# A decoder trunk with a top-2-of-8 expert layer: first-sweep row capacity of an expert 96 instead of 128

## What is computed

```python
def moe_swiglu(h, w_router, w_gate, w_up, w_down):
    logits = (x @ w_router)                       # x: 256 tokens x 1024
    top_logit, top_idx = lax.top_k(logits, 2)     # each token goes to 2 of 8 experts
    gates = softmax(top_logit)
    ...
    # expert e: ( silu(x_e @ w_gate[e]) * (x_e @ w_up[e]) ) @ w_down[e], 1024 -> 3584 -> 1024
    # out[token] += gate * y
```

## Time and profile before

| | us |
|---|---|
| median of 3 runs | 1450.31 (1448.35 to 1453.87) |
| the profiled execution, its own time | 1451.46 |
| its span, first to last instruction | 1449.7 |
| TensorE busy | 1418.1 (98%) |
| weight loads of TensorE | 1202.5 (83%) |
| VectorE busy | 1116.5 (77%) |
| ScalarE busy | 944.7 (65%) |
| mean granted TensorE clock | 0.993 of full |

### The profile page before, as it was taken

The page is one execution under the profiler, slowest core; times in us unless marked ns, Lnnn a source line. Parts: engine busy times, 40 slices in busy tenths (PEclk is TensorE's granted clock), DMA queues, the critical chain, the costliest instruction groups (busy, mean ns, idle before and its releaser), DMA issues.

```text
span 1449.7 us, 19532 instructions
## 1 busy us (share of the span) xinstructions
PE 1418.1 (98%) x7348; PEld 1202.5 (83%) x7348; DVE 1116.5 (77%) x865; ACT 944.7 (65%) x866; POOL 52.8 (4%) x78
## 2 busy tenths in 40 slices
PE   8999999999999999999999999999999999999997
PEld 8887899998887888888888888888888888888885
DVE  5565545456775898798888889879888888987987
ACT  5654444434664877687677777767768768677773
POOL 1000100000000500000000000000000000000002
PEclk9999999999999999999999999999999999999999
DMA  9734675555531599999999999999999999999993
GB/s 287 260 125 130 225 262 175 183 196 189 189 117 59 191 398 395 395 396 395 393 359 395 397 349 392 398 350 389 395 393 348 396 393 348 393 398 364 389 396 127
DMA packets 205253, 446.72 MB, mean 308 GB/s; under 512 B 8448, under 2 KB 42400, under 8 KB 205200
## 3 DMA queue, kind: packets, MB, share of 16 engines
q1 hardware_dynamic: 200144, 428.34, 80.3%
q0 software_dynamic: 5056, 17.66, 3.5%
HBM read 432.86 MB, written 13.11 MB: 308 GB/s over the span
## 4 chain that ended last, share of the span: by engine, by line
PE 91%; DVE 4%; ACT 3%; DMA 1%; issue 1%; SPq 1%; DVEq 0%; ACTq 0%
PE ps L1686 28%; PE ps L1688 28%; PE ps L1687 28%; PE ps L2300 2%; DMA raw<-in_w_mem_kv_dram 1%; ACT w_hi L593 1%; DVE w_lo L1058 1%; ACT sc L637 0%; PE ps L2294 0%; PE ps L1835 0%; DVE small L1105 0%; PE ps L1712 0%; DVE act_lo L1071 0%; PE ps L1804 0%; PE ps L2243 0%
## 5 line engine op out<-in xcount | busy, mean ns | idle before, releaser
L1567 DVE TENSOR_TENSOR e_wlo<-raw,e_whi 128x2048 fp32r<-128x2048 f32 x336 | 752.4, 2284 | 101.9 <-ACT e_whi L977 101.7
L977 ACT ACTIVATE e_whi<-raw 128x2048 fp32r<-128x2048 f32 x336 | 622.9, 1915 | 50.1 <-PE ps L1688 26.0
L1686 PE MATMUL ps<-e_whi,act_hi 128*128 128x512 f32 x1344 | 529.3, 394 | 0.9 <-DVE act_lo L1525 0.9
L1688 PE MATMUL ps<-e_wlo,act_hi 128*128 128x512 f32 x1344 | 523.9, 390 | 0.0
L1687 PE MATMUL ps<-e_whi,act_lo 128*128 128x512 f32 x1344 | 523.2, 389 | 0.0
L1688 PEld LDWEIGHTS ps<-e_wlo,act_hi 128*128 128x128 f32 x1344 | 252.3, 188 | 53.3
L1686 PEld LDWEIGHTS ps<-e_whi,act_hi 128*128 128x128 f32 x1344 | 252.5, 188 | 51.9 <-DVE act_lo L1525 1.3
L1687 PEld LDWEIGHTS ps<-e_whi,act_lo 128*128 128x128 f32 x1344 | 252.6, 188 | 50.7
L1058 DVE TENSOR_TENSOR w_lo<-raw,w_hi 128x2048 fp32r<-128x2048 f32 (+3 forms) x69 | 148.7, 2167 | 121.7 <-ACT w_hi L593 121.3
L593 ACT ACTIVATE w_hi<-raw 128x2048 fp32r<-128x2048 f32 (+3 forms) x69 | 124.3, 1816 | 50.5 <-PE ps L1688 46.2
L982 ACT ACTIVATE act_hi<-ps 128x512 fp32r<-128x512 f32 x56 | 33.5, 598 | 157.2 <-PE ps L2300 157.1
(11 more groups left out here) (270 smaller groups left out, 964.1 us busy)
## 6 DMA issues: line engine op xcount, KB each, us to landing
raw<-in_w_exp_gate_dram SPq DMA_DIRECT2D x112, 1024.0 KB, 9.2
raw<-in_w_exp_up_dram SPq DMA_DIRECT2D x112, 1024.0 KB, 9.6
raw<-in_w_exp_down_dram SPq DMA_DIRECT2D x112, 1024.0 KB, 10.3
raw<-in_w_dense_gate_dram SPq DMA_DIRECT2D x11, 1024.0 KB, 5.1
raw<-in_w_dense_up_dram SPq DMA_DIRECT2D x11, 1024.0 KB, 5.4
raw<-in_w_dense_down_dram SPq DMA_DIRECT2D x11, 1024.0 KB, 6.8
raw<-in_w_out_dram SPq DMA_DIRECT2D x8, 1024.0 KB, 4.9
raw<-in_w_in_a_dram SPq DMA_DIRECT2D x7, 1024.0 KB, 12.0
```

The lines of the kernel that those rows point to most:

```text
L977: nc.scalar.activation(e_whi[:, (s - NPRE) % E_SPLIT, :], raw[:, s % RAW, :], ACT.Copy)\
L1567: nc.vector.tensor_tensor(e_wlo[:, r, :], raw[:, s % RAW, :], e_whi[:, r, :].bitcast(F32), ALU.subtract).then_inc(lo_ready, 1)
L1686: nc.tensor.matmul(dst, l_hi, r_hi, start=start, stop=False)
L1688: return nc.tensor.matmul(dst, l_hi, r_lo, start=False, stop=stop)
```

## The change

The first sweep gives each expert 96 rows, and two further sweeps of 128 stand behind the same branch (ranks 96 to 223, and 224 on). The branch is taken when an expert has over 96 tokens.

```diff
+SWEEPS = 3
+CAP = (96, P, P)
+FIRST_RANK = (0, 96, 96 + P)
...
-    routed_rows = nc.dram_tensor("routed_rows", ((NE + 1) * P, D), F32).ap()
-    y_rows = nc.dram_tensor("y_rows", (NE * P, D), F32).ap()
+    routed_rows = nc.dram_tensor("routed_rows", ((NE + 1) * CAP[0], D), F32).ap()
+    y_rows = nc.dram_tensor("y_rows", (NE * CAP[0], D), F32).ap()
...
-                            sp.dma_start(x_rows, routed_rows[P:].rearrange("(e p) d -> e p d", p=P)[e])\
+                            sp.dma_start(x_rows[0:CAP[0], :],
+                                         routed_rows[CAP[0]:].rearrange("(e p) d -> e p d", p=CAP[0])[e])\
...
-            with sp.If(over > P):
+            with sp.If(over > CAP[0]):
...
-                pool.dma_start(y_rows[P * i:P * i + P, :], y_tok).then_inc(y_sent, 16)
+                pool.dma_start(y_rows[CAP[0] * i:CAP[0] * i + CAP[0], :], y_tok[0:CAP[0], :]).then_inc(y_sent, 16)
...
-                    nc.scalar.activation(h_hi[j % 2], ps[:, 4, :].rearrange("p (m n) -> p m n", m=4), ACT.Copy)\
+                    nc.scalar.activation(h_hi[j % 2][:, :, 0:cap],
+                                         ps[:, 4, :].rearrange("p (m n) -> p m n", m=4)[:, :, 0:cap], ACT.Copy)\
...
-                        nc.scalar.activation(e_h[:, :], ps[:, j % 2, :], ACT.Silu).then_inc(e_silu, 1)
+                        nc.scalar.activation(e_h[0:cap, :], ps[0:cap, j % 2, :], ACT.Silu).then_inc(e_silu, 1)
...
+            nc.vector.memset(oh[:, :, CAP[0]:P], 0.0)
...
-                            ins = nc.tensor.matmul(ps[:, 1 + 2 * half, P * k:P * k + P], H[:, t, c:c + P], select[:, t, :],
+                            ins = nc.tensor.matmul(ps[:, 1 + 2 * half, P * k:P * k + cap], H[:, t, c:c + P],
+                                                   select[:, t, 0:cap],
...
-                            ins = three(bank, xg_hi[:, k, :], xg_lo[:, k, :], hi[:, kk, :], lo[:, kk, :],
+                            ins = three(bank[0:cap, :], xg_hi[:, k, 0:cap], xg_lo[:, k, 0:cap], hi[:, kk, :], lo[:, kk, :],
...
-                            ins = nc.tensor.transpose(ps[:, 1 + 2 * half, P * k:P * k + P], x_rows[:, c:c + P], ident)
+                            ins = nc.tensor.transpose(ps[:, 1 + 2 * half, P * k:P * k + cap], x_rows[0:cap, c:c + P],
+                                                      ident[0:cap, 0:cap])
...
-                        ins = nc.tensor.transpose(ps[:, 4, P * m:P * m + P], e_h[:, P * m:P * m + P], ident)
+                        ins = nc.tensor.transpose(ps[:, 4, P * m:P * m + cap], e_h[0:cap, P * m:P * m + P],
+                                                  ident[0:cap, 0:cap])
...
-                                ins = three(ps[:, 5 + n, :], h_hi[j % 2][:, f, :], h_lo[j % 2][:, f, :], hi[:, m, ns],
+                                ins = three(ps[0:cap, 5 + n, :], h_hi[j % 2][:, f, 0:cap], h_lo[j % 2][:, f, 0:cap], hi[:, m, ns],
...
-            with pe.If(over > P):
-                for t in range(TT):
-                    scatter(0, t)
-                experts(1)
+            with pe.If(over > CAP[0]):
+                for sweep in range(1, SWEEPS):
+                    experts(sweep)
```

More of the change, by code:

```diff
@@ L948, in gathered, with evacuate_y @@
                     act.wait_ge(disp, sweep * 2 * NE + 2 * e + half + 1)
[L949 to L953, removed]
+                    nc.scalar.activation(xg_hi[:, 4 * half:4 * half + 4, 0:CAP[sweep]],
+                                         ps[:, 1 + 2 * half, :].rearrange("p (k n) -> p k n", k=4)[:, :, 0:CAP[sweep]],
+                                         ACT.Copy).then_inc(xg_h, 1)
+            def evacuate_y(i, sweep):
                 act.wait_ge(slot_used, (i + sweep * NE) * PER_EXPERT + NPRE)
@@ L1023, in _ @@
             over = act.value_load(flag[0:1, 0:1], min_val=0, max_val=S)
-            with act.If(over > P):
+            with act.If(over > CAP[0]):
                 act.wait_ge(y_sent, 16 * (NE - 1))
-                evacuate_y(NE)
-                experts(1)
-                act.wait_ge(slot_used, 2 * NE * PER_EXPERT + NPRE)
+                for sweep in range(1, SWEEPS):
+                    experts(sweep)
+                act.wait_ge(slot_used, SWEEPS * NE * PER_EXPERT + NPRE)
             prime(ACT.Sqrt)
@@ L1642, in experts @@
                 expert(NE - 1, True)
-                return remainder_y, add_tile
-            remainder_y, add_tile = experts(0)
+            experts(0)
             add_rows(0, 1)
@@ L1651, in _ @@
             last_gates = cur_gate.rearrange("p (t o) -> p t o", o=1)
-            with dve.If(over > P):
-                remainder_y(NE)
-                nc.vector.tensor_copy(last_gates, route_gate[:, :, NE:NE + 1]).then_inc(cur_done, 1)
+            with dve.If(over > CAP[0]):
+                nc.vector.tensor_copy(route_gate[:, :, 0:1], route_gate[:, :, NE:NE + 1]).then_inc(cur_done, 1)
                 dve.wait_ge(cur_done, 2)
-                for t in range(TT):
-                    add_tile(0, t)
-                experts(1)
-                dve.wait_ge(e_add, 4 * (NE + 1))
+                for sweep in range(1, SWEEPS):
+                    experts(sweep)
+                dve.wait_ge(e_add, 4 * (SWEEPS - 1) * NE)
             nc.vector.tensor_copy(last_gates, route_gate[:, :, NE:NE + 1]).then_inc(last_gate, 1)
@@ L2233, in _, with gather @@
             nc.tensor.matmul(ps[:, 4, 0:NE], ones[:, :], msk[:, 1, :], start=False, stop=True).then_inc(totals, 1)
-            def gather(select, ready=None):
+            def gather(select, cap, ready=None):
                 for half in range(2):
@@ L2356, in expert @@
                         pe.wait_ge(oh_ready, 2 * e + n_oh + 4)
-                        gather(oh)
+                        gather(oh, cap)
                     down(e, STEPS - 1, PER_EXPERT - 2, range(1) if last else range(2))
@@ L2364, in experts @@
                 expert(NE - 1, True)
-                return scatter
-            scatter = experts(0)
+            experts(0)
             over = pe.value_load(flag[0:1, 0:1], min_val=0, max_val=S)
-            with pe.If(over > P):
-                for t in range(TT):
-                    scatter(0, t)
-                experts(1)
+            with pe.If(over > CAP[0]):
+                for sweep in range(1, SWEEPS):
+                    experts(sweep)
             for n in range(2):
```

81 lines of the change are left out of this document (46 added, 35 removed).

## The result

| | before | after |
|---|---|---|
| median (lowest to highest), 11 runs each, us | 1450.65 (1448.35 to 1453.87) | 1453.52 (1451.16 to 1454.87) |
| ratio to before | | 1.0019, 95% interval 1.0012 to 1.0027 |
| the profiled execution, own time / span, us | 1451.46 / 1449.7 | 1451.16 / 1449.3 |

The change gives nothing: 2.9 us slower, 0.2%, which the interval tells from zero and which lies inside "the same". The forecast was 1429.3, and 1453.5 lies above its range. The profiled execution of after is the fastest of its 11, so its span hides the loss: its first gather starts at 480.24 us, where it starts at 483.26 before and at 480.2 to 482.7 in the other traces with after's code up to there. From the gather's start to the span's end the two take 966.4 and 969.1 us.

The account below looks back on a forecast made before the run. TensorE was taken to bound the expert layer, at 226.6 ns between matmul starts. Matmuls 13.4, transposes 7.1 and gather 0.5 sum to 21.0 us, taking the profiled 1451.46 to 1430.5 and the median to 1429.3; range 1425 to 1445.

Parts of the forecast that it names:

- (6): Weight and row transfers as the next limit: 114.1 of 116.0 us an expert, still fitting, costed at 0.
- (1): Expert layer's 4032 matmuls with 96 stationary columns: 3.3 ns less each, 13.4 us gained, bounds 0 and 13.4.
- (2): The 280 hidden and row transposes move 96 columns, not 128: 7.1 us gained, bounds 0 and 7.5.
- (3): First gather moves 96 columns in 16 products: 0.5 us gained, or 0 if loads set the pace.
- (4): ScalarE and VectorE copies shrink but TensorE covers them; TensorE's 0.3 us wait for VectorE stays; 0 for the extra memset.
- (5): Rows in and out fall from 0.52 to 0.39 MB each per expert; time gained only if (6) bites.
- (7): Kernel's end: VectorE's 2.93 us of issue at the jump over the branch stays.
- rival A: Transfers become the bound, an expert takes 117.9 us, 6 us gained: 1444.5 us; chance 0.08.
- B: The narrower stationary columns give nothing, only transposes and gather gain: 1442.7 us; chance 0.09.
- C: The transposes give nothing, only matmuls and gather gain: 1436.4 us; chance 0.06.
- Rival D: Stationary loads below 128 columns lose a fast path, 40 ns instead of 13.3 per matmul: 1550 us; chance 0.06.

Follow-up runs that it names:

- e2_only_matmuls: The kernel before with only the expert layer's 4032 matmuls narrowed to 96 stationary columns; 1461.95 us, 1.0082 of before.
- e4_micro: The kernel before plus 37 rows of 24 matmuls after TensorE's last wait, varying stationary count, block start and moving width; distances read, its time not compared.
- e8_micro2: The kernel before plus 39 other groups of 24 matmuls behind it, with other counts, starts and widths; distances 113.0 to 233.5 ns, no kernel time given.
- e1_mix128: The kernel after with the 4032 matmuls back at 128 stationary columns, rows and transposes still 96 wide; 1445.33 us, 0.9964 of before.
- e5_cap80_wide_gather: e3 with the first gather back at 128 moving columns; 1441.84 us, 0.9938 of before. Also written e5.
- e3: e1_mix128 with 80 rows instead of 96 in the first sweep, matmuls still 128 stationary columns; 1442.47 us, 0.9948 of before.
- e6_cols97: The kernel after with 97 stationary columns in the matmuls instead of 96; runs at 1452.97 and 1453.15 us against 1464.04 to 1465.43.
- e10_cap88: The kernel after with 88 rows and columns instead of 96; 1451.82 us, 1.0012 of before.

## Why the prediction was wrong, point by point

**What bounds the kernel: right.** TensorE without a gap, the chain on it, and the distance of starts as the price. That frame carried every result here: eight times the change in an expert's time gives the measured change within 2 us in every kernel with one distance. It misses the first expert, where weights are late (see (6)).

**(1) The matmuls: the step that failed.** It took -3.3 ns for each of 4032 matmuls, -13.4 us, from layer 0's m = 0 block, with bounds of 0 and 13.4. Measured: +3.3 ns in a settled row of them, and by e2_only_matmuls +10.5 us by the experts' distances (2.6 ns a matmul, with the slow ones behind the transposes), +11.2 in the time. The error was not the reading of the earlier trace rows but its carrying over to another moving width, which the last part named as the condition ("if the extra of 10 ns belongs to 256 moving columns only") and gave no chance. The bounds failed as well. The two values of layer 0, m = 0 and m = 1, were 3.3 ns apart by the block's start alone (e4_micro has 116.0 and 120.0 ns for the two, in one and the same bank). They were a sign that the extra depends on the form, and no row said that 128 columns pay the most; an honest upper bound had to lie above 0, say +13.4 for a step of the same size the other way. "10 ns is the floor" was read from 16 columns with 256 moving and does not hold there either: e8_micro2 has 113.0 ns, 6.3 over, for 16 to 80 columns. With 512 the least of over 40 forms is 13.3.

**(2) The transposes: right, and the size too.** 7.1 us forecast; 6.9 by e1_mix128's experts, 5.5 in its time, since the first expert waits. The bound that feared the stationary load does not bite: the transposes follow one another in 83 ns instead of 109.

**(3) The first gather: 0.5 us forecast, nothing came.** From its start to the first product it takes 5.3 us before, 5.5 after, 5.8 in e1_mix128, 6.8 with 80 moving columns, 5.4 in e5_cap80_wide_gather. The bound of 0 was the right one: the first half of the gather went from 3.33 to 3.28 us. The rest hangs on when the clock rises: with 80 columns it stays at half until 492 us.

**(4), (5) and (7): right but for a few tenths.** VectorE's wait shrank from 1.9 to 1.0 us instead of staying; no other engine shows on the chain of the later experts. VectorE's issue at the jump is 2.67 us before and 2.52 after, and in after it no longer lies on the chain, which gives about 0.4 us that was not forecast.

**(6) and rival A: the transfers do not bind from the second expert on.** They had no chance to be tested at 116.0 us an expert. At 117.41 us (e3) the experts' distance still follows TensorE's sum. In e1_mix128 at 117.77, ScalarE's waits for weights between 600 and 1400 us are 13.2 and 2.2 us in 23 times, and TensorE does not feel them. The first expert is another matter, which neither (6) nor A looked at: TensorE is idle there for 1.31 us in e1_mix128 and 1.21 in e5_cap80_wide_gather.

**Rivals B and C.** B said 226.6 ns and 1442.7: nearer than the forecast, and still one step of 3.3 ns too low; it too took a loss from narrow blocks to be impossible. C falls by e1_mix128.

**Rival D and the rule behind it.** D needed 253 ns a matmul; 96 columns take 230.0, and 127, 97, 95 and 88 columns took 226.5 to 227.0 in e4_micro, as 128 do. The Trainium skill, in "TensorE: Matmul & The Clock Gate", section "Weight-path perf modes — Fast Weight Load (FWL) and DoubleRow", ties the fast load to exactly 128 weights in a type other than FP32. If that rule decides anything here, its price is no more than a few ns: 127 columns cost the same as 128. That section of the Trainium skill gives its 32 cycles for fp8 and says that fp32 wins nothing, so their likeness to the 13.3 ns, which the prediction notes, shows nothing; the operands here are float32r, which the section does not name. It pointed at the right place, though, since the only loss of this change lies in the stationary block. D's sign was right and its mechanism and size were not.

**The range.** 1425 to 1445 was the sum's range plus rivals on one side only. With 4032 x ±3.3 ns, and the transposes' 7 us, it would have been 1429 to 1457, which holds the measured 1453.5.

## What to carry to other kernels

A price per instruction that multiplies by thousands must come from a row with the same form in every dimension: the stationary count, its start and the moving width. Where only a neighbour is in the trace, the sign is open too; a row of 24 such instructions appended to the kernel is a first answer, but 97 and 88 columns, and 96 from column 32, took other values in the layer than alone, so only the kernel itself settles it. Narrow what moves (transposes, rows copied). With 512 moving columns leave the stationary block at 128: no narrower one was faster in any run, and going back from 96 to 128 gave 8 us (e1_mix128 against after). And look at the first pass of a loop by itself: its loads can be late where those of the later passes are not.

## What the runs showed of the hardware

- The distance between matmuls with 512 moving columns is 226.5 to 234.5 ns, by count and start of the stationary block, with no order in the count: 128 take 227.0, 127 take 227.0, 120 take 233.5, 96 take 230.0, 88 take 227.0, 80 take 233.0 (e4_micro). The loads of 96 columns are busy for less (page of after: 1089.2 us against 1202.5), and this buys nothing.
- Some forms have more than one value, taken anew behind the transposes and kept for tens of matmuls: 97 columns put the same kernel at 1453 or at 1464 to 1465 us and show 226.7, 230.0 and 233.3 ns in one trace (e6_cols97); 88 columns show 226.7, 231.1 and 233.3 (e10_cap88). 128 and 96 columns from multiples of 128 floats settle at 226.7 and 230.0 in every step.
- With 256 moving columns 16 to 80 stationary columns take 113.0 ns, 96 take 116.0 from columns 0 and 64 and 120.0 from column 32, 128 take 120.0 (e4_micro, e8_micro2).
- A transpose of 96 rows and 96 moving columns has a record of 245 ns, one of 128 by 128 274 ns; from one start to the next it is 83 ns instead of 109 (70 with 80 columns, e3), and four of them with their neighbours take 0.09 us less.
- A narrower gather can be slower: with 80 instead of 128 moving columns its record is 7.08 us instead of 5.61, and the granted clock is still 0.50 at 490 us, where it is 1.00 in e5 (e3, e5; the trace with 88 columns, e10_cap88, is like e3's).
